# A hybrid decoder layer: the h products of two gate tiles moved between the last steps of two attention stages

## The reference

```
h = rmsnorm(x, norm_g[0]) * (1 + sc1) + sh1
z = h @ w_in                       # mixers' inputs, and g: 4 * 1024 gate columns
y_a = short_conv(a_u, a_b, a_c)    # branch A
y_d = dsa(...)                     # branch D: top-256 keys by an indexer, then attention
y_f = fox(...)                     # branch F: forgetting attention
y_s = swa(...)                     # branch S: window of 128 keys, with sinks
proj = einsum('blnc,ncd->blnd', stack([y_a, y_d, y_f, y_s]), w_branch)
y = sum(sigmoid(g) * proj, axis=branch) @ w_o
x = x + g1 * rmsnorm(y, norm_g[1])
... then a SwiGLU channel mixer with the same norms
```

## Time and profile before

| | |
|---|---|
| median of 3 runs | 1764.03 us (1760.74 to 1764.3) |
| profiled execution, its own time | 1760.8 us |
| span of its trace | 1759.0 us |
| PE busy | 1672.6 us, 95% of the span |
| mean granted TensorE clock | 0.988 of full speed |

### The profile page before, as it was taken

How to read it: one execution, slowest core, us unless ns; L and a number is a source line. 1 busy time by engine, 2 the same in 40 slices (tenths; PEclk the granted TensorE clock), 3 DMA queues, 4 the chain that set the end, 5 groups by cost and what they waited for, 6 DMA issues and landing times.

```text
span 1759.0 us, 22694 instructions
## 1 busy us (share of the span) xinstructions
PE 1672.6 (95%) x8036; PEld 1394.4 (79%) x8036; DVE 1044.9 (59%) x1746; ACT 595.5 (34%) x1054; POOL 821.6 (47%) x537
## 2 busy tenths in 40 slices
PE   2899999999999999989999999999999999999996
PEld 2787878787888888879888788888888888888884
DVE  5714835656999999947577345743453354345438
ACT  1533336264222222246323354323223222322323
POOL 0621130102446565520388423766558556755664
PEclk9999999998999999999999999999999999999998
DMA  8222141010111111240674511121112011201213
GB/s 288 86 60 60 40 110 42 31 36 32 47 58 45 45 45 51 105 102 1 221 271 160 203 61 48 37 72 48 48 48 72 25 63 55 65 30 48 72 69 158
DMA packets 37166, 138.87 MB, mean 79 GB/s; under 512 B 4592, under 2 KB 4592, under 8 KB 37104
## 3 DMA queue, kind: packets, MB, share of 16 engines
q1 hardware_dynamic: 34864, 130.70, 21.7%
q0 software_dynamic: 2240, 7.34, 1.9%
HBM read 118.10 MB, written 13.63 MB: 75 GB/s over the span
## 4 chain that ended last, share of the span: by engine, by line
PE 80%; DVE 8%; DMA 4%; issue 3%; ACT 3%; POOL 2%; SPq 0%; DVEq 0%; POOLq 0%; ACTq 0%
PE ps L612 23%; PE ps L614 23%; PE ps L613 23%; PE ps L811 4%; PE ps L790 2%; DMA region_b<-in_w_ada 2%; DVE y_f L2179 1%; PE ps L716 1%; DVE y_f L2148 1%; PE ps L717 1%; DVE region_a L2133 1%; ACT y_t L1407 1%; PE ps L642 1%; DMA raw<-in_w_ffn 1%; DVE region_a L2206 1%
## 5 line engine op out<-in xcount | busy, mean ns | idle before, releaser
L612 PE MATMUL ps<-h_t,w_t 128*128 128x512 f32 x1112 | 437.4, 393 | 0.6 <-POOL w_t L1500 0.4
L614 PE MATMUL ps<-h_t,w_t 128*128 128x512 f32 x1112 | 433.6, 390 | 0.0
L613 PE MATMUL ps<-h_t,w_t 128*128 128x512 f32 x1112 | 433.5, 390 | 0.0
L612 PEld LDWEIGHTS ps<-h_t,w_t 128*128 128x128 f32 x1112 | 209.4, 188 | 45.2 <-issue 2.4
L614 PEld LDWEIGHTS ps<-h_t,w_t 128*128 128x128 f32 x1112 | 209.2, 188 | 44.1
L613 PEld LDWEIGHTS ps<-h_t,w_t 128*128 128x128 f32 x1112 | 209.4, 188 | 42.9 <-issue 0.7
L1500 POOL TENSOR_TENSOR w_t<-raw,w_t 128x1280 fp32r<-128x1280 f32 (+1 forms) x50 | 141.6, 2832 | 196.0 <-ACT w_t L1097 195.7
L2148 DVE TENSOR_TENSOR y_f<-ps,y_f 128x512 f32<-128x512 f32 x120 | 80.7, 686 | 217.5 <-PE ps L614 217.5
L1649 POOL TENSOR_TENSOR w_t<-raw,w_t 128x512 fp32r<-128x512 f32 x80 | 110.2, 1383 | 144.5 <-ACT w_t L1388 144.4
L1833 DVE MAX8 top<-region_b 128x8 f32<-128x384 f32 (+5 forms) x192 | 157.9, 881 | 17.3 <-issue 16.7
L1836 DVE MATCH_REPLACE8 region_b<-top,region_b 128x384 f32<-128x384 f32 (+5 forms) x192 | 166.1, 876 | 0.0
(11 more groups left out here) (266 smaller groups left out, 3264.6 us busy)
## 6 DMA issues: line engine op xcount, KB each, us to landing
region_b<-in_w_ada SPq DMA_DIRECT2D x48, 512.0 KB, 4.5
raw<-in_w_ffn SPq DMA_DIRECT2D x46, 512.0 KB, 3.7
raw<-in_w_gates SPq DMA_DIRECT2D x32, 640.0 KB, 3.9
region_d<-in_w_ffn SPq DMA_DIRECT2D x20, 512.0 KB, 4.2
raw<-in_w_z SPq DMA_DIRECT2D x18, 512.0 KB, 3.6
region_a<-in_x SPq DMA_DIRECT2D x8, 512.0 KB, 11.6
raw<-in_w_o SPq DMA_DIRECT2D x8, 512.0 KB, 3.6
region_b<-in_x SPq DMA_DIRECT2D x8, 512.0 KB, 6.6
```

What stands on the lines that cost most here:

```text
L612: pe.matmul(o, a_hi, m_hi, start=first, stop=False, skip_group_check=more)
L613: pe.matmul(o, a_hi, m_lo, start=False, stop=False, skip_group_check=more)
L614: return pe.matmul(o, a_lo, m_hi, start=False, stop=last, skip_group_check=more)
```

## The change

Two gate tiles, T and T+1, get their h products among the last steps, in sixteen parts; the second tile's stand in banks 6 and 7, the logits banks of odd units. A table says how many parts stand at each of six places (1, 2, 2, 2, 3, 3), and the rest (three) come behind the last `turn_out`. Behind the stage `gates_begun` makes the branch products of both tiles, four halves in banks 2 and 3. ACT and POOL split tile T+1 earlier: ACT at the fifth unit of the attention stage, POOL as soon as ACT has done it, ahead of its work on the first gate tile. Tile T+2 is split where it was: behind ACT's two halves of tile T, and on POOL behind both halves of tile T too.

```
+FILL = (1, 2, 2, 2, 3, 3)
...
-                beside = gate_beside(gate)
+                beside = gates_beside(gate)
...
+                def fill(parts):
+                    for _ in range(parts):
+                        next(beside, None)
...
                     turn(u)
                     if u >= end - 2:
-                        next(beside)
+                        fill(FILL[2 * (u - end + 2)])
                     if u - 2 >= u0:
                         turn_out(u - 2)
                     if u > u0:
                         values(u - 1)
                     if u >= end - 2:
-                        next(beside)
+                        fill(FILL[2 * (u - end + 2) + 1])
+                fill(FILL[4])
                 turn_out(end - 2)
                 values(end - 1)
-                next(beside)
+                fill(FILL[5])
                 turn_out(end - 1)
-                for _ in beside:
-                    pass
...
+                fill(4 * KT)
...
+                for j in range(2):
+                    T = T0 + j
+                    pe.wait_ge(s_w_lo, T + 1)
...
+                            product(ps[:, 4 + 2 * j + half, :], w_t[:, T % 2, 0, w], w_t[:, T % 2, 1, w], h_hi[:, k, c],
...
+            def gates_begun(T0, buf):
+
+                for T in (T0, T0 + 1):
+                    for half in range(2):
+                        if T > T0:
+                            pe.wait_ge(s_zf, 2 * T + half - 1)
+                        tile_half(ps[:, 2 + half, :], T % 2, half, KT, BT, y_hi(buf), y_lo(buf)).then_inc(s_z, 1)
...
-            gate_first(T_AFS, 0)
-            gate_tile(T_AFS + 1, 0)
+            gates_begun(T_AFS, 0)
...
-            gate_first(T_GD, 1)
-            gate_tile(T_GD + 1, 1)
+            gates_begun(T_GD, 1)
```

On ACT:

```
+                    if gate is not None and u == u0 + 4:
+                        split_hi(gate + 1, n=GT)
...
-                split_hi(T0 + 1, n=GT)
                 gate_tile(T0, m0, bank=4)
                 split_hi(T0 + 2, n=GT)
-                gate_tile(T0 + 1, m0 + 2)
+                gate_tile(T0 + 1, m0 + 2, bank=6)
```

On POOL:

```
+            split_lo(T_AFS + 1)
...
-            gate_pairs(T_AFS, True)
+            gate_tile(T_AFS, 0, True)
+            split_lo(T_AFS + 2, n=GT)
+            gate_tile(T_AFS + 1, 1, True)
...
-            for j in range(2):
-                split_lo(T_GD + j + 1, n=GT)
-                if j == 1:
-                    pool.wait_ge(s_refill[0], 48)
-                gate_tile(T_GD + j, j, False)
+            split_lo(T_GD + 1)
+            gate_tile(T_GD, 0, False)
+            split_lo(T_GD + 2, n=GT)
+            pool.wait_ge(s_refill[0], 48)
+            gate_tile(T_GD + 1, 1, False)
```

More of the change, by code:

```diff
@@ L842, in attention, with gates_beside @@
                     if u >= end - 2:
-                        next(beside)
+                        fill(FILL[2 * (u - end + 2) + 1])
+                fill(FILL[4])
                 turn_out(end - 2)
                 values(end - 1)
-                next(beside)
+                fill(FILL[5])
                 turn_out(end - 1)
-                for _ in beside:
-                    pass
[L851 to L855, removed]
-                    return
[L857 to L869, removed]
+                fill(4 * KT)
+            def gates_beside(T0):
+                if T0 is None:
+                    return
+                for j in range(2):
+                    T = T0 + j
+                    pe.wait_ge(s_w_lo, T + 1)
+                    for half in range(2):
+                        for k in range(KT):
+                            c, w = slice(half * HALF, (half + 1) * HALF), slice(k * P, (k + 1) * P)
+                            product(ps[:, 4 + 2 * j + half, :], w_t[:, T % 2, 0, w], w_t[:, T % 2, 1, w], h_hi[:, k, c],
+                                    h_lo[:, k, c], k == 0, k == KT - 1)
+                            if k % 2:
+                                yield
+            def gates_begun(T0, buf):
+                for T in (T0, T0 + 1):
+                    for half in range(2):
+                        if T > T0:
+                            pe.wait_ge(s_zf, 2 * T + half - 1)
+                        tile_half(ps[:, 2 + half, :], T % 2, half, KT, BT, y_hi(buf), y_lo(buf)).then_inc(s_z, 1)
             z_group(T_FOX, 2)
@@ L1220, in exponentials, with attention @@
                                    accum_out=den[:, g % 4, col:col + 1]).then_inc(s_exp, 1)
-            def attention(u0, n):
+            def attention(u0, n, gate=None):
                 end = u0 + n
@@ L1245, in _ @@
             z_group(T_SWA, T_AFS - T_SWA)
-            attention(U_FOX + 2 * TT, 2 * TT + TT)
+            attention(U_FOX + 2 * TT, 2 * TT + TT, T_AFS)
             act.wait_ge(s_ya_in, 16 * BT)
@@ L1292, in _ @@
             z_group(T_DSA, T_GD - T_DSA)
-            attention(U_DSA, HEADS * TT)
+            attention(U_DSA, HEADS * TT, T_GD)
             gate_pairs_begun(T_GD, 6 * KT, KT // 2 - 1)
@@ L1582, in _ @@
             pool.tensor_tensor(y_lo(0), ya_back[:, :, :], y_hi(0).bitcast(F32), ALU.subtract).then_inc(s_ya, 1)
-            gate_pairs(T_AFS, True)
+            gate_tile(T_AFS, 0, True)
+            split_lo(T_AFS + 2, n=GT)
+            gate_tile(T_AFS + 1, 1, True)
+            with order.loop(KT // 2 - 1, 0) as i:
+                for j in range(2):
+                    split_lo(T_AFS + 2 + j + 1, i, 2, GT)
+                    gate_tile(T_AFS + 2 + j, 2 + j, True, i)
             pool.wait_ge(s_ys_hi, 1)
```

## The result

The changed kernel took 1772.23 us (median of 6 runs, 1768.35 to 1774.78), the kernel before, run beside it, 1761.85 us (6 runs, 1759.04 to 1764.3). The ratio is 1.0057 with a 95% interval of 1.0044 to 1.0069: slower by 10.0 us, 7.8 to 12.2. The forecast was 1770.5 us, slower.

What follows compares the result with a forecast made beforehand. PE, busy 95% of the span, was taken as the bound. Terms -3.5 (SWA) + 8.0 (DSA) + 2.0 (clock) + 0 (early splits) gave +6.5 us: 1767.3 beside the profiled execution, 1770.5 beside the median, range 1763.5 to 1777.

Steps and rivals of the forecast that it cites:

- SWA's wait goes: End of SWA stage: PE's 3.45 us wait for DVE's division and the 4.3 us lost to half clock vanish, -7.8.
- What is late next: the chain over one `sig` and one `prj`: Behind SWA: ACT and POOL's chain makes PE wait 1.1 and 3.1 us; the place gains 3.5 of 7.8 us.
- DSA's end: Behind the DSA stage: tile T_GD+2 starts later, +6.6 to some +10 us, taken as +8.0.
- The load stands beside the chain: Load of tile T_GD+2 moves to at most 879.2, ahead of the top of the chain's range by a microsecond.
- The clock behind the DSA wait: Half clock behind PE's new DSA wait of some 5 us: +1.7 to +4.3, taken as +2.0.
- The clock behind SWA's new wait: Behind SWA's new 3.1 us PE wait: no clock loss, 0, at most +1.7.
- the `diag` wait of 3.0 us: PE's wait at `diag` in the old profile, followed by clock 1.00; taken as nearest to SWA's new wait.
- The early splits: ACT's and POOL's splits moved to the fifth unit: taken as 0, up to 4.2 us a stage if uncovered.
- the first (both chains covered): Both stages: -7.8 us with nothing given back, and the 0.42 as well, 1755.8 us; chance 0.08.
- The second: New waits short and clock high, or SWA's relief larger: +3.1, 1767.1 us, no difference to be told; chance 0.2.
- The third: Early splits cost too, POOL's subtraction meeting DVE's bias operation: +6.5 + 4.2, 1774.7 us; chance 0.1.
- the fourth: SWA's wait only moves to the last `turn_out`, so -7.8 fails: 1778.3 us; chance 0.07.

Runs made afterwards that it cites:

- e7: Kernel before, with POOL's subtraction for branch A's output made to wait for DVE's last division of the SWA stage: 1755.59 us, ratio 0.9961.
- e3: Kernel before, with only the second gate tile's early splits on ACT and POOL, all products where they were: 1762.46 us, ratio 0.9994.
- e8: Change at the SWA stage alone, last four of sixteen parts held behind the first tile's branch products; DSA stage as before: 1753.28 us, ratio 0.9942.
- e4: Changed kernel with the load of tile T_GD+2 issued ahead of the adaLN loads: 1769.86 us, ratio 1.0051 against the kernel before.
- e5: Changed kernel with the last four parts at the DSA stage held behind tile T_GD's branch products: 1768.14 us, ratio 1.0040 against the kernel before.
- e6: Changed kernel with four DSA parts held back and the load of tile T_GD+2 issued early: 1765.09 us, ratio 1.0023 against the kernel before.
- e1: Kernel before with the change at the SWA stage alone, DSA stage as before: 1759.92 us, ratio 0.9987.
- e9: The changed kernel run once more for a second trace: 1770.24 us, ratio 1.0050 against the kernel before.
- e11: Changed kernel with four parts held back at both stages and the load of tile T_GD+2 early: 1758.54 us, ratio 0.9987 against the kernel before.
- e10: SWA change alone with its last four parts held, plus POOL's branch A subtraction waiting for DVE's last division: 1752.45 us, ratio 0.9939 against before.
- e2: Kernel before with the change at the DSA stage alone, SWA stage as before: 1771.86 us, ratio 1.0048.

## Why the prediction was right, and where it was off

The forecast was +6.5 us beside the profiled execution; the change's own stretches give +8.2, the runs +10.0 (7.8 to 12.2). So the direction and the mechanism were right and the size was 1.7 to 3.5 us too small; the time itself, 1772.23 against 1770.5, came closer because the kernel before ran at a median of 1761.85 this time, 2.2 us under the 1764.03 that the forecast was added to. Step by step, as the prediction put them:

- **SWA's wait goes (-7.8).** Right: no wait at L825 at 426.20, clock 1.00 from 417 to 430. That DVE's addition is slow because of POOL's subtraction is shown by e7. The size holds for the trace of before alone; the half clock in it ended 3 us later than in e3.
- **What is late next: the chain over one `sig` and one `prj`.** Right. The waits were forecast as 1.1 and 3.1 us after SWA and came as 0.92 and 2.65; tile T_AFS+2 came 3.8 us earlier against its stage, forecast 3.5, and in five more traces the stretch from the first moved matmul on is the same within 0.01 us. e8 shows that this chain is the cause: 24 matmuls in front of it give the rest back.
- **DSA's end (+8.0).** Right: +7.77. The waits were forecast as 2.5 and 4.8 to 8, and came as 2.55 and 5.30. From the branch products' start to POOL's last sum it took 9.93 us (878.32 - 868.39), 9.62 before, so the four operations slowed down less than feared; the split, which the prediction kept at 2.93, took 3.86. That the sum came out is partly luck: 6.6 was worked out, and of the 1.4 put on it for slow operations ahead of the split 0.3 was there, and 0.9 was in the split. In e4 it is the other way round (POOL's last sum 2.29 us, its split 2.87), with the same DSA stretch of 37.04.
- **The load stands beside the chain.** Right as put: e4 changes nothing. But it stood 1.1 us ahead of the chain only, and so it keeps most of the loss once the chain is out of the way: 4.9 us, e5's 35.61 less e6's 30.73. A cure for one alone is worth 0 (e4) or 1.4 us (e5), both 6.3.
- **The clock behind the DSA wait (+2.0, 1.7 to 4.3).** +2.6 measured, within the bounds.
- **The clock behind SWA's new wait (0, at most +1.7).** This is the step that was mis-sized. It was taken from the `diag` wait of 3.0 us, behind which the trace of before had 1.00. Measured +1.7, in five of the six traces with that wait (after, e1, e5, e6, e9; not in e4, where it was 2.65 us too). The row that it leant on was an exception: behind the `diag` wait (2.96 to 3.69 us) the clock stayed at 1.00 in the traces of before and e11, whose block took 2.05 us, and the block took 2.60 to 3.78 in the other eleven. One row of one trace was taken to say which way a thing goes that goes either way.
- **The early splits (0, up to 4.2 a stage).** Right: e3 at 0.9994, by a margin of 0.5 us (forecast 0.35) between POOL's split and DVE's bias operation.

Of the rivals, the first (both chains covered) is what e8 makes of the SWA place, with 24 matmuls more; it did not happen by itself. The second needed the clock to stay high behind both waits. The third falls with e3, and the fourth with the timeline: no wait stands at the last `turn_out`. The runs say 1.8 us more than the change's stretches; that lies within their interval, and no cause is claimed for it.

## What to carry to other kernels

Before filling an engine's idle time with work from later, look at what that work was covering where it stood: here 60 matmuls hid a chain of ACT and POOL that is 8 us long at one place and 14 at the other, and at the second there was no idle time to fill. Move only as much as the chain behind leaves over (e8 moved four parts less and gained 10 us where e1 gained 2.3). And ask first why the wait is there: one instruction put off on another engine (e7) gave 7 us without moving any product.

## What the runs showed of the hardware

- A DVE addition of two SBUF operands, 128 x 4 elements, takes 0.16 us alone and 2.8 to 4.1 us beside a POOL subtraction of 128 x 2048, until that one ends. POOL pays too, and who began first decides it. At tile T_GD+2 POOL's split of 128 x 1280 took 2.87 to 2.95 us in six traces, where it began 0.03 to 0.85 us ahead of an adaLN sum of DVE (before, e1, e3, e4, e5, e10), and 3.86 to 3.99 us in five, where such a sum had begun 0.08 to 0.63 us ahead of it (after, e2, e7, e8, e9); e6 and e11 have 3.35.
- The granted clock behind a short wait of PE is not a function of its length. Behind 2.03 us it stayed at 1.00 in e6 and fell to half in e11; behind 2.65 us it stayed in one trace and fell in five; behind 2.88 it stayed (e6); behind 3.0 us it stayed in before and fell in after; behind the same 3.45 us the half clock ended at 426.6 in one trace and at 429.66 in another. What it cost went from 0.6 us (the `diag` block of e3, 2.60 us for 2.05) to 4.3.
- The same load of tile T_GD+2, issued by SP behind the same four adaLN loads, was there for ACT 4.7 to 5.1 us later in eight traces (4.7 in e5, 4.9 in after), 6.1 before and 7.2 in e7. In e7 this made the DSA stage's end 0.9 us longer, and POOL's split behind it another 1.0.
- The fall can come after PE has started again. Behind the wait that ended at 446.22 the first matmuls ran at full speed, and the slow ones began at 447.82 (records 0.63 us long in place of 0.39, 0.43 apart in place of 0.23):

```profile
446.55 0.39 PE L616 MATMUL ps<-h_t,w_t 128*128 128x512 f32 x1
...
447.46 0.56 PE L617 MATMUL ps<-h_t,w_t 128*128 128x512 f32 x1
447.82 0.63 PE L615 MATMUL ps<-h_t,w_t 128*128 128x512 f32 x1
```
